# Hymba trunk layer: banded attention blocks with the scores issued a block ahead and the second memory copy on ScalarE

## The reference

```python
x = x + 0.5 * swiglu(rmsnorm(x, g_ffn1), ...)
proj = rmsnorm(x, g_mix) @ w_in            # u | gate | q | k | v
lru_out = rmsnorm(rg_lru(u) * gelu(gate), g_lru_out)
# swa_prompt: blocks of 128 queries against their own and the previous 128 keys, 8 heads of 64, 2 kv heads
s = einsum('nbqkgd,nbskd->nbkgqs', qb, kk) * HEAD_DIM ** -0.5
p = sink_softmax(s, mask, sink)            # one more exp(sink) in the denominator
o = einsum('nbkgqs,nbskd->nbqkgd', p, vv)
x = x + concat([lru_out, rmsnorm(attn_o, g_attn_out)]) @ w_out
mk, mv = rmsnorm(mem, g_mem) @ w_ck, rmsnorm(mem, g_mem) @ w_cv   # memory_kv, 256 memory tokens
x = x + cross_attend(rmsnorm(x, g_xattn), mk, mv)
x = x + 0.5 * swiglu(rmsnorm(x, g_ffn2), ...)
```

## Time and profile before

| what | value |
|---|---|
| median of three runs | 2483.44 us |
| the profiled execution's own time | 2480.83 us |
| its span, first to last instruction | 2479.0 us |
| PE busy in the span | 2333.8 us, 94% |
| DVE, POOL, ACT busy | 1431.7, 1029.9, 444.1 us |
| chain that ended last, by engine | PE 85%, DVE 6%, POOL 5%, ACT 3% |
| granted TensorE clock, mean | 0.973 |

### The profile page before, as it was taken

The page is one execution under the profiler, slowest core; times in us unless marked ns, Lnnn a source line. Parts: engine busy times, 40 slices in busy tenths (PEclk is TensorE's granted clock), DMA queues, the critical chain, the costliest instruction groups (busy, mean ns, idle before and its releaser), DMA issues.

```text
span 2479.0 us, 35690 instructions
## 1 busy us (share of the span) xinstructions
PE 2333.8 (94%) x13994; PEld 2070.5 (84%) x13994; DVE 1431.7 (58%) x1864; ACT 444.1 (18%) x908; POOL 1029.9 (42%) x717
## 2 busy tenths in 40 slices
PE   6999999999999999688789989999999999999997
PEld 5899998999998887556578977889998999999896
DVE  7755555655555775876454324447655655565564
ACT  5111100110110416233322013231000000000002
POOL 2543443434433164546635430344434434344333
PEclk9999999999999999899889999999999999999998
DMA  4111101111010010201211134011011110110102
GB/s 142 69 40 45 47 20 51 51 51 51 34 42 26 26 43 26 97 28 58 71 55 48 34 137 170 26 59 69 21 47 51 51 51 35 50 40 28 68 0 74
DMA packets 40285, 131.89 MB, mean 53 GB/s; under 512 B 5799, under 2 KB 11047, under 8 KB 37799
## 3 DMA queue, kind: packets, MB, share of 16 engines
q1 hardware_dynamic: 37280, 127.80, 14.8%
q10 hardware_dynamic: 2951, 3.35, 0.4%
HBM read 123.33 MB, written 7.81 MB: 53 GB/s over the span
## 4 chain that ended last, share of the span: by engine, by line
PE 85%; DVE 6%; POOL 5%; ACT 3%; issue 1%; DMA 1%; POOLq 0%; SPq 0%; DVEq 0%; ACTq 0%
PE ps L552 27%; PE ps L554 26%; PE ps L553 26%; POOL w_hi L452 2%; POOL w_lo L453 1%; PE ps L961 1%; PE ps L914 1%; DVE act_lo L1315 1%; DVE rstd L1302 1%; DVE mem_raw L1544 1%; PE ps L737 1%; PE ps L578 0%; ACT sq L1003 0%; DVE y L1825 0%; ACT act_hi L1018 0%
## 5 line engine op out<-in xcount | busy, mean ns | idle before, releaser
L552 PE MATMUL ps<-act_hi,w_hi 128*128 128x288 f32 (+1 forms) x1968 | 658.0, 334 | 48.0 <-DVE act_lo L1315 34.8
L553 PE MATMUL ps<-act_lo,w_hi 128*128 128x288 f32 (+1 forms) x1968 | 653.1, 332 | 0.0
L554 PE MATMUL ps<-act_hi,w_lo 128*128 128x288 f32 (+1 forms) x1968 | 652.6, 332 | 0.0
L552 PEld LDWEIGHTS ps<-act_hi,w_hi 128*128 128x128 f32 x1968 | 377.5, 192 | 81.9 <-issue 38.6
L553 PEld LDWEIGHTS ps<-act_lo,w_hi 128*128 128x128 f32 x1968 | 377.6, 192 | 29.6
L554 PEld LDWEIGHTS ps<-act_hi,w_lo 128*128 128x128 f32 x1968 | 377.0, 192 | 29.1
L452 POOL TENSOR_TENSOR w_hi<-w_raw,ones 128x256 fp32r<-128x256 f32 x216 | 193.9, 898 | 472.2 <-PE ps L554 440.0
L1358 DVE SCALAR_TENSOR_TENSOR x<-ps,x 128x288 f32<-128x288 f32 (+1 forms) x504 | 263.6, 533 | 188.0 <-PE ps L554 172.8
L552 PE MATMUL ps<-hid_hi,dn_hi 128*128 128x288 f32 (+1 forms) x1056 | 348.7, 330 | 3.6 <-issue 3.6
L554 PE MATMUL ps<-hid_hi,dn_lo 128*128 128x288 f32 (+1 forms) x1056 | 347.7, 329 | 0.0
L553 PE MATMUL ps<-hid_lo,dn_hi 128*128 128x288 f32 (+1 forms) x1056 | 347.7, 329 | 0.0
(11 more groups left out here) (244 smaller groups left out, 2934.3 us busy)
## 6 DMA issues: line engine op xcount, KB each, us to landing
w_raw<-in_w_ffn SPq DMA_DIRECT2D x66, 512.0 KB, 3.7
w_raw<-in_w_plain SPq DMA_DIRECT2D x54, 512.0 KB, 3.6
ff_raw_up<-in_w_ffn SPq DMA_DIRECT2D x44, 512.0 KB, 4.4
ff_raw_down<-in_w_ffn SPq DMA_DIRECT2D x22, 512.0 KB, 6.4
ck_T<-in_ck SPq DMA_DIRECT2D x8, 1024.0 KB, 7.7
cv_n<-in_cv SPq DMA_DIRECT2D x8, 1024.0 KB, 4.9
x<-in_x SPq DMA_DIRECT2D x2, 1152.0 KB, 11.0
x<-in_x SPq DMA_DIRECT2D x1, 2048.0 KB, 12.0
```

The costliest lines, as they stand in the source:

```text
L552: pe.matmul(out, wh, ah, start=(first and n == 0), stop=False)
L553: pe.matmul(out, wh, al, start=False, stop=False)
L554: ins = pe.matmul(out, wl, ah, start=False, stop=end)
```

## The change

Three edits, and the waits that they need:
- TensorE issues the scores of block b+2 at the end of block b, behind `weigh(b, 1)` and ahead of `turn_v(b + 1)`, and no longer the scores of b+1 at its start. The scores of block 1 stand ahead of the loop.
- VectorE copies only memory tile 0 of a block. The copy stands behind the maxima of b+1 and ahead of rope(b+2), staging v and the probabilities.
- ScalarE copies memory tile 1 of a block, behind the exponentials of b+1 and ahead of its copy of v. In block 7 there are no exponentials, and the copy stands behind the p_T copies and ahead of the four stores and the samples' exponentials.
- Two waits on `kv_ev` are added, on TensorE ahead of the cross attention and on ScalarE ahead of the stores of mem_k and mem_v.

```diff
@@ TensorE, block_step
-                if more:
-                    scores(b + 1)
                 pe.wait_ge(p_done, b + 1)
                 turn_p(b, s, 0)
...
                 memory_tile(b, s, 1)
                 weigh(b, 1).then_inc(pv_mm, 1)
+                if rot:
+                    scores(b + 2)
                 if more:
                     turn_v(b + 1)
...
             turn_v(0)
+            scores(1)
             pe.wait_ge(memn_lo_done, 1)
...
             pe.wait_ge(x_tab, 16)
+            pe.wait_ge(kv_ev, 2 * NB + 1)
@@ ScalarE
+            def take_memory(b, s):
+                act.wait_ge(mem_mm, b * 2 + 2)
+                if s == 0:
+                    to = mem_kT[:, bass.ds(b + 1, 1), :].squeeze(1)
+                else:
+                    to = mem_v[:, 1, bass.ds(b * P - P, 2 * P)]
+                act.activation(to, ps[:, 7, 256:512], ACT.Copy).then_inc(kv_ev, 1)
...
                 if more:
                     exps(b + 1, 1 - s)
+                take_memory(b, s)
+                if more:
                     take_v(b + 1, 1 - s)
...
+            act.wait_ge(kv_ev, 2 * NB + 1)
             act.dma_start(t_out["mem_k"], mem_kT[:, :, :]).then_inc(stored, 16)
@@ VectorE
-            def take_memory(b, s, j):
-
-                dve.wait_ge(mem_mm, b * 2 + j + 1)
+            def take_memory(b, s):
+
+                dve.wait_ge(mem_mm, b * 2 + 1)
                 if s == 0:
-                    to = mem_kT[:, bass.ds(b + j, 1), :].squeeze(1)
+                    to = mem_kT[:, bass.ds(b, 1), :].squeeze(1)
                 else:
-                    to = mem_v[:, j, bass.ds(b * P - P, 2 * P)]
+                    to = mem_v[:, 0, bass.ds(b * P - P, 2 * P)]
...
                 maxima(b + 1, 1 - s, steps)
+                take_memory(b, s)
                 if rot:
                     rope(b + 2, s, steps)
                 stage_v(b + 1)
-                for j in range(2):
-                    take_memory(b, s, j)
                 probabilities(b + 1, 1 - s, steps)
...
-            take_memory(NB - 1, 1, 0)
+            take_memory(NB - 1, 1)
...
                 dve.tensor_tensor(st8[:, 2, 0:4], st8[:, 1, 0:4], c_("sink_s", 0, 4), ALU.add).then_inc(s_nmax, 1)
-            take_memory(NB - 1, 1, 1)
```

## The result

| | before | after |
|---|---|---|
| median of 20 runs each, us | 2483.07 (2481.05 to 2485.80) | 2487.64 (2485.23 to 2492.24) |
| ratio after / before, 95% interval | | 1.0022 [1.0016, 1.0029] |
| profiled execution: own time / span, us | 2480.83 / 2479.0 | 2487.27 / 2485.5 |
| first turned probabilities start, us | 1069.44 | 1072.00 |
| the eight blocks, from there to the end of the last memory tile, us | 145.4 | 141.9 |

The kernel became slower by about 4.6 us, 0.18% by the medians and 0.22% by the ratio. The interval lies wholly above 1, so it is slower, but by no more than about the 0.2% that the prediction had called no change; the median lies inside the range given. The span of the profiled execution grew by 6.5 us.

What follows compares the result with a forecast made beforehand. The loop was taken as bound by GpSimd's weight splits and TensorE's odd-block memory tiles, one behind the other. Terms -6.0 + 0.5 + 5.0 + 2.1 + 1.1 = +2.7 us gave a median of 2486.1, range 2480.5 to 2492.

Steps and rivals of the forecast that it cites:

- Part 1: TensorE's scores issued a block ahead in the loop: worth nothing, as TensorE is ready 3.6 us before GpSimd.
- Part 2: Copies in the loop: three odd-block collisions of normalisation and GpSimd splits go, -6.0 us; block 0's rope costs +0.5.
- rival 2: Odd-block collisions stay because the normalisation starts only as GpSimd does: 6.0 us more, +8.7, 2492.1; chance 0.07.
- block 0's rope: Block 0: behind the first copy the rope lies wholly over GpSimd's splits, +0.5 us, between 0 and 1.9.
- Part 3: Last block: the copy holds stores and exponentials, samples' probabilities 5.0 us late; TensorE's clock then falls, 2.1 us more.
- Part 4: TensorE's clock ahead of odd blocks' first tiles: half a chance of 2.2 us in pair 1, so +1.1.
- Rival 1: The clock falls ahead of all four odd tiles: 5.3 in place of 1.1 us, +6.9, 2490.3; chance 0.20.
- 3 (the clock holds): The clock holds in the loop and in the tail: -4.0 us, 2479.4; chance 0.10.
- 4 (the late exponentials are absorbed): The samples' late exponentials are absorbed further down, so the tail costs nothing: -4.4 us, 2479.0; chance 0.08.

Runs made afterwards that it cites:

- e5: e1 with the scores of block b+1 back at the start of block b, as in before; 2481.24 us, ratio 0.9991.
- e4: e1 with VectorE's normalisation made to wait in every block for that block's second memory tile, as in before; 2484.51 us, ratio 1.0010.
- e12: e1 with VectorE's normalisation waiting for the second memory tile in even blocks alone; 2476.91 us, ratio 0.9980.
- e1: The kernel after, with ScalarE's very last memory tile copy moved behind the samples' exponentials; 2480.51 us, ratio 0.9995.
- e2: The kernel before, with only the last memory tile's copy moved to ScalarE ahead of the stores, and the two kv_ev waits; 2489.65 us, ratio 1.0028.
- e3: The kernel after, with the four stores issued behind the samples' exponentials; 2482.96 us, ratio 1.0001.
- e10: The kernel after, with 23 products nobody reads on TensorE ahead of the samples' transposes; 2488.00 us, ratio 1.0020.
- e6: e1 with both memory tile copies on VectorE, the second behind the probabilities, the last behind the samples' probabilities; 2481.17 us, ratio 0.9992.
- e7: e1 with 28 products nobody reads on TensorE ahead of each odd block's first memory tile; 2483.68 us, ratio 1.0004.

## Why the prediction was right

**Part 1, scores: nothing.** Right. From a second tile's end to the turning of the probabilities 4.0 us were forecast; in after it is 3.9 (1101.74 to 1105.62), in before it was 4.0. e5 puts the scores' place between nothing and 0.6 us.

**Part 2, copies: -6.0 + 0.5 us.** Right. The loop less the clock's share fell by 6.1 (142.0 to 135.9) where 5.5 net were forecast, and e4 and e12 show that it hangs on the odd blocks' three normalisations. They miss the splits by 0.02 us, so the up to 0.1 left of each collision was fairly priced. It was also close: the "2.2 us of room" held against rival 2 is the lead of the normalisation's start, and the normalisation itself takes 2.29, so by these figures there was no room, and the prediction's sum (its end at E+5.15, GpSimd at E+5.1) says so as well. The 0.5 for block 0's rope was 0.3: there GpSimd's sixteen splits took 14.81 us from first to last (1078.80 to 1093.61), where before they took 14.55 (1076.09 to 1090.64). The Trainium skill, page SBUF — State Buffer, section SBUF: two separate sides, calls VectorE's and GpSimd's shared port an exclusive lock for the whole of an instruction. The trace agrees where the instruction is long: the 2.77 us split is 0.72 and 2.05 more, nearly all of the 2.29 that a normalisation takes by itself, and in e4 VectorE's took 2.58, as if it had in turn waited for the split it met. On the size for short instructions the trace does not agree with what the prediction took from the page: block 0's rope would have cost GpSimd all 1.9 us, and it cost 0.3. Splits beside it took 1.05 to 1.07 and 0.79 in place of 0.73.

**Part 3, last block: +5.0 and +2.1 us.** Right in both. From the last tile's end to the transposes it was 2.2 and became 7.4 us: +5.1. From the transposes to the result it was 12.2 and became 14.4: +2.2. e1, e2 and e3 show the cause, e10 recovers 1.7 of the second term by the clock alone. For the clock the prediction had taken its upper bound, and that came true.

**Part 4, clock in the loop: +1.1 us.** This is the term that was mis-sized: it was +2.6 (the four tiles took 6.0 us above 3.12 each, where it was 3.4). The gaps came out nearly as worked out (3.1, 4.0, 4.0 and 2.2 forecast; 2.9, 4.2, 4.2 and 2.5 measured), but it was not the first pair's tile that fell slow, to which I had given half a chance, but the last one's, which I had called safe. The two misses, 1.1 too much and 2.3 too little, partly cancel, which is luck. Rival 1 thus came half true. My reading of the earlier trace rows, that tiles are slow behind 3.6 us and fast behind 1.0, left all between open, and I filled it with the length of the gap alone. That was wrong: in the same execution 2.5 us was followed by a slow tile and 2.9 by a fast one.

**The rest.** The sum was +2.7; the loop and tail measured +3.8, the difference being Part 4's 1.5 and Part 3's 0.2 less Part 2's 0.6. The median came out at 2487.6 where 2486.1 was forecast. It moved by 4.6 us, so some 0.8 of it lie in neither. The prediction gave 0.55 to a time within 0.2% of before and 0.35 to a slower one; the result lies on the line between the two. Rival 2 (collisions stay), 3 (the clock holds) and 4 (the late exponentials are absorbed) are each contradicted by a row above. The change is thus two things that nearly cancel. With its last copy moved behind the exponentials it is worth -1.7 us by e1's medians, not told from nothing. In the profiles the clock took back 2.6 of the 6.1.

What stays open: why the odd tile of the first pair is slow in some profiles and fast in others with the same work and gap (in e5 the scores stand elsewhere, but e6 has after's order on TensorE), whether that is a matter of the kernel at all or of the single execution, and where the 2.6 us before the first block come from.

## What to carry to other kernels

An instruction moved in an in-order queue takes along everything behind it: the store issues too, and above all in the last turn of a loop, where there is no next turn's work for it to stand behind. When a step makes TensorE wait a little longer for a late engine, add the clock to the bill: here a gap that grew from 1.0 to 2.5 us made the next 3.1 us of products 5.5. Where such a gap can't be closed, products that nobody reads can fill it: here 12 of them, 2.9 us in all, brought back all of it, and 28, which ran past what the gap waits for, lost more than they won (e7). Look first whether the gap can be made small again by order alone, as e12 did ahead of block 7.

## What the runs showed of the hardware that was not expected

- The gap alone does not tell the clock. Idle time ahead of the four odd first tiles, and the tile's length, from the profiled executions:

```
after           2.95 -> 3.1    4.25 -> 4.6    4.24 -> 5.3    2.48 -> 5.5
e5_scores_back  2.80 -> 4.4    4.11 -> 5.5    4.12 -> 5.5    2.50 -> 5.5
e6_all_vector   2.96 -> 4.6    4.25 -> 5.5    4.25 -> 5.5    2.30 -> 5.5
e12_held_even   2.82 -> 3.1    4.13 -> 4.6    4.10 -> 5.5    1.01 -> 3.1
```

  In these runs a gap of 1.0 us was followed by a tile at full clock and one of 2.3 to 2.5 or of 4.1 and more never (though the tile's first products could still be fast); behind 2.8 to 3.0 both were seen. The gaps of 2.3 to 2.5 are all ahead of block 7, so it may be the place and not the length that decides there. But e2 has a slow tile (4.5 us) behind 2.15 us in block 5, and ahead of the second tile of its block 4 a gap of 1.99 was followed by 4.6 us, where in before the same gap (2.01) in the same place was followed by 3.1.
- A product of two f32 tiles of 128x128 shows as two records and takes 0.23 to 0.25 us (56 records in 6.52 us, 24 in 2.94 us); in before a transpose of such a tile by the identity comes every 0.11 to 0.13 us.
- VectorE and GpSimd lengthen each other. Beside block 0's rope in after, splits took 1.05 to 1.07 us in place of 0.73, and the rope's own instructions 1.12 and 0.82 us, where in before's block 1, with GpSimd idle, they took 0.69 and 0.28.
- Four small store issues in ScalarE's queue hold the activations behind them for 3.26 us, but run beside the activations when they stand behind them (the issue at 1214.33 in e3, among the exponentials).
